# Expert weights loaded in four large ring parts with 32 KB and 16 KB runs, in place of twelve slots with 8 KB runs

## The reference, cut to what matters

```python
D_MODEL, N_EXPERTS, TOP_K, D_EXPERT = 1024, 32, 4, 1024

def encoder_layer(x, ...):
    h = rms_norm(x, norm_mix_g)
    mix, ... = token_mixers(h, ...)          # gated delta rule || conformer convolution, then w_out
    x = x + mix
    h = rms_norm(x, norm_ffn_g)
    return x + moe_ffn(h, ...)

def moe_ffn(h, w_router, b_router, w_gate_up, b_gate_up, w_down, b_down):
    logits = h @ w_router + b_router
    top_val, top_idx = lax.top_k(logits, TOP_K)
    gates = softmax(top_val)
    ...                                      # for each expert e, on its rows xblk of h:
        gu = xblk @ w_gate_up[e] + b_gate_up[e]      # w_gate_up[e]: 1024 x 2048 f32, 8 MB
        x_glu, x_lin = split(gu, 2)
        x_glu, x_lin = minimum(x_glu, 7.0), clip(x_lin, -7.0, 7.0)
        act = x_glu * sigmoid(1.702 * x_glu) * (x_lin + 1.0)
        y = act @ w_down[e] + b_down[e]              # w_down[e]: 1024 x 1024 f32, 4 MB
    ...                                      # y, times the gate, is added to the rows it belongs to
```

## Time and profile before

| | |
|---|---|
| median of 3 runs | 1297.71 us (1296.84 to 1298.78) |
| profiled execution | 1296.87 us, its span 1295.1 us |
| PE busy in the span | 1197.0 us (92%) |
| HBM read | 428.50 MB, 402.65 MB of it weights of experts |
| weight loads | 256 of w_gate_up and 128 of w_down, 1024 KB each |
| mean granted TensorE clock | 0.977 of 2.4 GHz |

### The profile page before, as it was taken

The page is one execution under the profiler, slowest core; times in us unless marked ns, Lnnn a source line. Parts: engine busy times, 40 slices in busy tenths (PEclk is TensorE's granted clock), DMA queues, the critical chain, the costliest instruction groups (busy, mean ns, idle before and its releaser), DMA issues. The chain is left out here.

```text
span 1295.1 us, 17190 instructions
## 1 busy us (share of the span) xinstructions
PE 1197.0 (92%) x6556; PEld 560.7 (43%) x6556; DVE 451.3 (35%) x887; ACT 241.8 (19%) x426; POOL 78.7 (6%) x81
## 2 busy tenths in 40 slices
PE   6999979998999999999999899899999999998986
PEld 3666669855543433323232324434343332323332
DVE  2989633224553223231312222321323322131224
ACT  2134425323201101010111101011110101111012
POOL 1100144154000000000000000000000000000000
PEclk9989989798899999999999999999999999999999
DMA  9321210016999999999999999999999999999994
GB/s 377 152 86 72 87 25 2 9 58 256 395 380 420 421 422 422 421 422 423 422 422 422 421 422 421 393 363 421 422 422 422 422 422 422 423 422 421 420 422 202
DMA packets 62153, 433.76 MB, mean 335 GB/s; under 512 B 7744, under 2 KB 8128, under 8 KB 11968
## 3 DMA queue, kind: packets, MB, share of 16 engines
q1 hardware_dynamic: 59696, 428.65, 80.4%
q0 software_dynamic: 800, 3.08, 0.6%
q10 hardware_dynamic: 1616, 1.45, 0.4%
HBM read 428.50 MB, written 4.65 MB: 334 GB/s over the span
## 5 line engine op out<-in xcount | busy, mean ns | idle before, releaser
L1835 PE MATMUL bank<-ring,win 128*64 128x512 f32 x1984 | 451.6, 599 | 44.9 <-DMA ring<-in_w_gate_up 44.9
L1835 PEld LDWEIGHTS bank<-ring,win 128*64 128x64 f32 x1984 | 135.0, 137 | 343.9 <-issue 206.6
L1855 PE MATMUL bank<-ring,win 128*64 128x512 f32 x992 | 222.6, 602 | 0.3 <-issue 0.3
L1303 DVE TENSOR_SCALAR win<-bank 128x512 f32<-128x512 f32 x33 | 22.8, 691 | 408.6 <-PE bank L1835 386.7
L1855 PEld LDWEIGHTS bank<-ring,win 128*64 128x64 f32 x992 | 70.3, 138 | 134.3 <-issue 131.1
L802 ACT ACTIVATE win<-win 128x512 f32<-128x512 f32 x33 | 20.8, 630 | 453.9 <-DVE win L1303 453.9
L810 ACT ACTIVATE win<-bank 64x512 f32<-64x512 f32 x64 | 37.8, 591 | 280.7 <-PE bank L1855 266.5
L1816 PE MATMUL bank<-qkvc,win 128*128 128x512 bf16 x288 | 67.7, 380 | 1.9 <-DVE xt L1297 1.9
L1237 DVE TENSOR_TENSOR win<-win,qkvc 128x1024 f32<-128x1024 f32 x16 | 19.6, 1226 | 143.0 <-ACT qkvc L828 143.0
L1297 DVE TENSOR_TENSOR xt<-xt,bank 128x512 f32<-128x512 f32 x108 | 68.0, 681 | 2.7 <-PE bank L1810 2.1
L937 DVE SCALAR_TENSOR_TENSOR cb<-ring,par,cb 128x384 f32<-128x384 f32 x120 | 66.7, 611 | 0.8
(11 more groups left out here) (305 smaller groups left out, 1083.0 us busy)
## 6 DMA issues: line engine op xcount, KB each, us to landing
ring<-in_w_gate_up SPq DMA_DIRECT2D x256, 1024.0 KB, 25.9
ring<-in_w_down SPq DMA_DIRECT2D x128, 1024.0 KB, 23.5
win<-in_w_in SPq DMA_DIRECT2D x3, 2048.0 KB, 7.3
ring<-in_w_in SPq DMA_DIRECT2D x2, 2048.0 KB, 13.5
win<-in_w_out SPq DMA_DIRECT2D x2, 2048.0 KB, 8.6
win<-in_w_in SPq DMA_DIRECT2D x4, 512.0 KB, 10.5
out_ss<-ring POOLq DMA_DIRECT2D x1, 2048.0 KB, 9.4
hT<-in_xT SPq DMA_DIRECT2D x2, 768.0 KB, 6.8
```

The lines of the kernel that those rows point to most:

```text
L1303: dve.tensor_scalar(g_s, bank[low], LIMIT, None, ALU.min).then_inc(g, 1)
L1835: mm = pe.matmul(bank[half][a * BLK:(a + 1) * BLK], xs[:, k], ring[:, c:c + 512], start=False, stop=(k == KD - 1), skip_group_check=True)
L1855: mm = pe.matmul(bank[7][a * BLK:(a + 1) * BLK], actT[:, (k % 4) * P + (k // 4) * BLK:][:, 0:BLK], ring[:, c:c + 512], start=(k == 0), sto ...
```

## The change

The ring is cut into four parts in place of twelve slots: two gate-up parts of 4 MB (4 slots each) and two down parts of 2 MB (2 slots each). A partition's rows in a part are neighbours in HBM: part r of gate-up holds rows r x 512 to r x 512 + 511, and partition p has rows 4p to 4p + 3 of them, a run of 32 KB. A down part has 4 rows of 4 KB in each partition, a run of 16 KB. There is one load for each part, one landing semaphore and one release. Expert 0 is loaded in six pieces (`FIRST_PIECES`), in the places of the ring and in the order of before; `EXTRA` counts them in the waits. The last part of the last expert is loaded in two halves, the second with a semaphore of its own.

Since row group k is now every fourth row of 512, the other operand must be picked in the same way. `h_parts` are written in the new order by ACT and DVE, which read h with a step of 16 bytes (`h2q`); `first_rows` reads h itself in this way; `a_rows` steps by 16 bytes, where it stepped by 8.

```diff
-SLOT_OF = (6, 7, 5, 0, 1, 2, 3, 4, 8, 9, 10, 11)
-FIRST_ORDER = (0, 1, 2, 8, 9, 3, 4, 5, 6, 7, 10, 11)
+GU, DN = 2, 2
+GQ, DQ = KD // GU, KD // DN
+NPART = GU + DN
+PART_AT = tuple(x * SLOT for x in (4, 0, 8, 10))
+FIRST_PIECES = ((0, 1, 4), (2, 0, 4), (1, 0, 2), (1, 2, 4), (0, 0, 1), (3, 0, 4))
+EXTRA = [16 * (sum(x[0] == r for x in FIRST_PIECES) - 1) for r in range(NPART)]
...
+        h2q = h2.rearrange("p (n r x q) -> p n r q x", n=NT, r=GU, q=GQ)
-        a_rows = a_s.rearrange("p (b r two) -> p b r two", b=2, two=2)
+        a_rows = a_s.rearrange("p (r q) -> p q r", q=DQ)
...
-        USED = (1, 2, 3, 4, 5, 6, 7, 11, 12, 13, 14, 16)
-        USES, GATE_UP_DONE, DOWN_DONE = 16, 11, 16
+        USED = [r + 1 for r in range(GU - 1)] + [GU + 3, GU + 4, GU + 6]
+        USES, GATE_UP_DONE, DOWN_DONE = GU + 6, GU + 3, GU + 6
...
+            def load_piece(ld, e, r, q0, q1, done=None):
+                if r < GU:
+                    rows_of, width, src = GQ, 2 * F, w_gate_up[bass.ds(e, 1), r * GQ * P:(r + 1) * GQ * P, :]
+                else:
+                    rows_of, width = DQ, D
+                    src = w_down[bass.ds(e, 1), (r - GU) * DQ * P:(r - GU + 1) * DQ * P, :]
+                src = src.rearrange("a (p q) n -> (a p) (q n)", q=rows_of)
+                ld.dma_start(ring[:, PART_AT[r] + q0 * width:PART_AT[r] + q1 * width], src[:, q0 * width:q1 * width])\
+                  .then_inc(done or s_w[r], 16)
+            def load_expert(ld, e, value):
+                for r in range(NPART):
+                    ld.wait_ge(s_wu, value(r))
+                    load_piece(ld, e, r, 0, GQ if r < GU else DQ)
...
-                            mm = pe.matmul(out, h_parts[j][:, n, k * P:(k + 1) * P], hits[:, n, 0:width],
+                            mm = pe.matmul(out, h_parts[j][:, n, k // GQ, k % GQ], hits[:, n, 0:width],
...
-                                       h23[:, n, k * P:(k + 1) * P], hp0[:, n], start=(n == 0), stop=(n == NT - 1))
+                                       h2q[:, n, k // GQ, k % GQ], hp0[:, n], start=(n == 0), stop=(n == NT - 1))
...
                 for k in range(KD):
-                    pe.wait_ge(s_w[SLOT_OF[k]], turn * 16 + 16)
+                    r, q = divmod(k, GQ)
+                    if q == 0:
+                        pe.wait_ge(s_w[r], turn * 16 + (16 + EXTRA[r]))
...
-                    if k < KD - 1:
+                    if q == GQ - 1 and k < KD - 1:
                         mm.then_inc(s_wu, 1)
```

More of the change, by code:

```diff
@@ L311, in stream_step @@
         s_tabs = sem("tables_ready")
-        s_w = [sem(f"w_landed{i}") for i in range(NSLOT)]
-        s_wu = sem("w_used")
+        s_w = [sem(f"w_landed{i}") for i in range(NPART)]
+        s_wu, s_whalf = sem("w_used"), sem("w_landed_last_half")
         s_xg4, s_xg5, s_xt4, s_xt5 = (sem(x) for x in ("rows_gathered_low", "rows_gathered_high", "rowsT_low", "rowsT_high"))
@@ L467, in _ @@
                             load_expert(sp, ei, lambda s: i * USES + ((NE - 4) * USES + USED[s]))
-            for e in (NE - 3, NE - 2, NE - 1):
+            for e in (NE - 3, NE - 2):
                 number = sp.value_load(expert_no[0:1, e:e + 1], min_val=0, max_val=NE - 1)
                 load_expert(sp, number, lambda s: n_extra * USES + ((e - 1) * USES + USED[s]))
+            number = sp.value_load(expert_no[0:1, NE - 1:NE], min_val=0, max_val=NE - 1)
+            for r in range(NPART):
+                sp.wait_ge(s_wu, n_extra * USES + ((NE - 2) * USES + USED[r]))
+                load_piece(sp, number, r, 0, GQ if r < GU else DQ // 2 if r == NPART - 1 else DQ)
+            load_piece(sp, number, NPART - 1, DQ // 2, DQ, s_whalf)
             for n in TILES:
@@ L817, in h_split @@
                 for n in TILES:
-                    act.activation(h_parts[0][:, n], h23[:, n], ACT.Copy).then_inc(s_up, 1)
+                    act.activation(h_parts[0][:, n], h2q[:, n], ACT.Copy).then_inc(s_up, 1)
                 act.wait_ge(s_lg, NT)
@@ L821, in h_split @@
                     act.wait_ge(s_lo, n + 1)
-                    act.activation(h_parts[1][:, n], h23[:, n], ACT.Copy).then_inc(s_up, 1)
+                    act.activation(h_parts[1][:, n], h2q[:, n], ACT.Copy).then_inc(s_up, 1)
             def y_split(u):
@@ L1844, in turn_act, with down @@
                 for j in range(4):
-                    mm = pe.transpose(bank[6][:, j * P:(j + 1) * P], a_rows[:, j // 2, :, j % 2], mat("ident"))
+                    mm = pe.transpose(bank[6][:, j * P:(j + 1) * P], a_rows[:, j], mat("ident"))
                 mm.then_inc(done, 1)
-            def down(turn, atr, n_atr):
+            def down(turn, atr, n_atr, last=False):
                 pe.wait_ge(atr, n_atr)
                 for k in range(KD):
-                    if k % 2 == 0:
-                        pe.wait_ge(s_w[KD + k // 2], turn * 16 + 16)
+                    j, q = divmod(k, DQ)
+                    if q == 0:
+                        pe.wait_ge(s_w[GU + j], turn * 16 + (16 + EXTRA[GU + j]))
+                    if last and k == KD - DQ // 2:
+                        pe.wait_ge(s_whalf, 16)
                     for a in range(2):
-                        c = (KD + k // 2) * SLOT + (k % 2) * D + a * 512
-                        mm = pe.matmul(bank[7][a * BLK:(a + 1) * BLK], actT[:, (k % 4) * P + (k // 4) * BLK:][:, 0:BLK],
+                        c = PART_AT[GU + j] + q * D + a * 512
+                        mm = pe.matmul(bank[7][a * BLK:(a + 1) * BLK], actT[:, q * P + j * BLK:][:, 0:BLK],
                                        ring[:, c:c + 512], start=(k == 0), stop=(k == KD - 1), skip_group_check=True)
@@ L1858, in down @@
                             mm.then_inc(s_wu, 1)
-                    if k % 2 == 1 and k < KD - 1:
+                    if q == DQ - 1 and k < KD - 1:
                         mm.then_inc(s_wu, 1)
@@ L1927, in wide_unit @@
                 for k in range(KD):
-                    pe.wait_ge(s_w[SLOT_OF[k]], WIDE * 16 + 16)
+                    r, q = divmod(k, GQ)
+                    if q == 0:
+                        pe.wait_ge(s_w[r], WIDE * 16 + 16 + EXTRA[r])
                     for x in range(2):
@@ L1931, in wide_unit @@
                             for a in range(2):
-                                c = SLOT_OF[k] * SLOT + half * F + a * 512
+                                c = PART_AT[r] + q * SLOT + half * F + a * 512
                                 mm = pe.matmul(bank[4 * x + half][a * BLK:(a + 1) * BLK], xTe[:, k, x * BLK:(x + 1) * BLK],
@@ L2019, in _ @@
             turn_hits(hp, BLK)
-            down(turn, s_atr, item + 1)
+            down(turn, s_atr, item + 1, last=True)
             pe.wait_ge(s_gtc, NU)
```

45 lines of the change are left out of this document (18 added, 27 removed).

## The result

The changed kernel takes 1304.18 us (median of 13 runs, 1300.06 to 1307.23) against 1297.71 (13 runs, 1294.72 to 1298.95): **a ratio of 1.0055, 95% interval 1.0044 to 1.0066**, 6.5 to 7.1 us slower. Its profiled execution took 1301.27 us with a span of 1299.5 (before 1296.87 and 1295.1). That one lies in the lower part of its runs, so the two traces show 4.4 us of the difference, and what the other runs had more is in no trace.

What follows compares the result with a forecast made beforehand. The stream of weights was taken as the bound, in a chain with PE through expert 16 and PE's tail. The end 6.2 us late plus 0.9 for the clock, 7.1 us on the median 1297.71, gave 1304.8 us; range 1297 to 1312.

Steps and rivals of the forecast that it cites:

- Long runs: Weight streams: 32 KB runs at 431.5 GB/s, 0.6 us saved per expert, 16.2 us over 27 experts.
- (a) Expert 0's start: First gate-up: stepped reads in first_rows cost 4.3 us (0 to 6.8), covering a 0.8 us late landing; start at 337.5.
- (b) Expert 1: Experts 1 and 2: parts freed and landed later, all of expert 2 at 409.4 against 403.5; start phase loses 5.9 us.
- (c), (d) The wide expert: Expert 16 starts 4.5 us later, at 801.1; the stream stands about 17 us against 8, losing its 2.5 us lead.
- The stop that was to be seen about 840: Sign to look for at the wide expert: a stop of 10 us in the GB/s line.
- (e) The end: Last weights land at 1267.7, four rows remain for PE, gate-up ends at 1274.6: 6.2 us late, same tail behind.
- (f) The clock: After long waits PE's clock may halve; counted only at experts 15 and 31, 0.9 us, range 0 to 3.6.
- Some 28 waits of 2 to 3 us, more in total than 44.9: Sign to look for: PE's waits at gate-up's second part, in place of 83 short waits totalling 44.9 us.
- stepped reads are not free: Denies the rival that stepped reads of h cost nothing, which gave 1300.3 us; chance 0.23.
- a rate of 435: Rival in the streams: long runs cost nothing of their own, 434.9 GB/s, 8.4 us less, 1296.4 us; chance 0.12.
- 32 KB runs are single packets: Denies a case of the does-less rival: runs cut into 16 KB packets, +4 us; that rival's chance 0.14.
- the distance in HBM: Rival in gate-up loads: partitions reading 32 KB apart cost 3.6 us an expert, about 1400 us; chance 0.03.

Runs made afterwards that it cites:

- short_coarse: Changed kernel with its parts, waits and releases, but each transfer cut by rows into 8 KB runs; 1319.19 us, 1.0180 of the kernel before.
- contig: Changed kernel with first_rows reading h without the 16-byte step (some values then wrong); 1300.64 us, 1.0030 of the kernel before.
- short_fine: Changed kernel's row order and stepped reads, but twelve 1 MB pieces per expert with 8 KB runs, waited for and released singly; 1301.46 us, 1.0042 of the kernel before.
- start: Changed kernel with 1 MB pieces in experts 0 and 1, no step in first_rows, release by 1 MB; 1300.13 us, 1.0032 of the kernel before.
- wide: Changed kernel with 1 MB pieces in experts 0 and 15 to 18, their pair 17/18 written out, release by 1 MB; 1299.34 us, 1.0027 of before.
- mix: Changed kernel with 1 MB pieces in experts 0, 1, 15 to 18, 31, no step in first_rows, 17/18 written out; 1294.50 us, 0.9982 of before.
- mix3: mix with expert 30 also in 1 MB pieces and a second pair of experts written out ahead of the loop; 1289.51 us, 0.9951 of the kernel before.

## Why the prediction was right

The forecast was 1304.8 us, the median 1304.18. The chain of costs and its places are borne out by the experiments. That the number is met to within 1 us is luck in part: for the two traces that the working is about it was 2.7 us too high (7.1 against 4.4), and within it several errors cancel. Step by step:

- **Long runs.** 431.5 GB/s was extrapolated for 32 KB; the changed kernel's windows show 431 and 430. The gain of 16.2 us was measured as 16.2 between short_coarse and the changed kernel. The intervals of the two ratios (1.0164 to 1.0196 and 1.0044 to 1.0066) leave some 2.5 us to either side of that.
- **(a) Expert 0's start.** first_rows took 11.47 us in place of 7.17, the 4.3 that was chosen between 0 and 6.8. It started 1.4 us earlier than in the trace of before, so gate-up began at 336.50 instead of 337.5. The two ways to measure the step's price at the end give 3.2 (contig) and 5.4 us (short_fine), each with an uncertainty of some 2. The size was met by luck, for the reading behind it does not hold. The 0.157 us between the starts of the transposes is raised by the first of each four, whose matmul takes 385 ns where the others take 284; the others start 0.121 apart, against 0.110 for the plain rows, so 0.011 and not 0.047 was there to be doubled. And the doubling does not come: the four transposes of 16-byte rows (L1861) still take 0.75 us, so 0.2 us for each group should have been 0. What first_rows pays is 0.12 us a pass at full clock, and it comes to 4.3 only because a third of the passes ran at half clock in the kernel before, where the step adds 0.02. The passage of the Trainium skill that the prediction names ("SBUF — State Buffer", section "Door 1: The DMA port swizzle") has lines of 16 bytes and two reads of a line for full rate, and goes on to call a stride of 4 fp32 free, which is 16 bytes. By the first part 8 bytes are free and 16 pay, by the second 16 are free: at full clock first_rows agrees with the first (329 ns against 192) and contradicts the second. The transposes, 0.121 at both steps, show no further cost from 8 to 16 bytes; whether it is the step at all that sets them apart from the plain rows, no run isolates.
- **(b) Expert 1.** Landings at 356.8 (forecast 356.6) and, for expert 2's part 0, 390.4 (389.9). Both hide two errors each. Expert 0's gate-up began 1.0 us early, but TensorE was at half clock again at its start (0.50 in 336.5:338; 15.13 us in place of 13.90), so its first part was freed at 344.6, not 344.4. Expert 1's gate-up began at 369.12, 1.6 us before the 370.7 forecast, but the load behind it took 14.0 us from issue to landing where 12.2 were worked out. 4.7 us of stream were missing by 460 where 5.9 less the first gain, about 5, were forecast. Without the step the coarse parts alone cost little here, 1.7 us by short_coarse against short_fine and nothing measurable by start against contig.
- **(c), (d) The wide expert.** It started at 800.05 (forecast 801.1) and expert 17 at 855.14 (856.8). By the bytes moved in 780:900 (404 and 332 GB/s, two windows of 60 us) the stream stood 120 - 44.2 MB / 431 = 17.5 us, as forecast, against 7 us before (417 and 379; the forecast had 8). The stop that was to be seen about 840, 10 us long, is there: from 839 to 849 next to nothing moves. The two windows of the changed kernel:

```profile
780.00:840.00 60.00, 56.01 (x374) 25.14 (x376) 17.71 (x31) 5.78 (x8) 0.00 (x0) 1.00 0.96 404
840.00:900.00 60.00, 59.42 (x356) 23.70 (x354) 15.26 (x29) 8.39 (x13) 0.00 (x0) 1.00 0.81 332
```

- **(e) The end.** Expert 31's part 1 landed at 1265.7, 2.0 us earlier than forecast, and gate-up ended at 1273.0 instead of 1274.6; 4.4 late, not 6.2. Of the 2.0, 1.5 is that expert 17 freed its part earlier. The tail behind it is the same, as forecast: the last down ends at 1285.2 us, 12.2 behind the end of gate-up, and in the kernel before at 1280.8, also 12.2; from the landing of the last weights it is 9.7 us (forecast 11) and was 4.3 (the forecast had 6). The whole forecast of the trace (7.1) was thus 2.7 too high, 1.8 of it here and 0.9 in the clock, and the runs' medians lie closer to it than the trace does.
- **(f) The clock.** 0.9 us were put in for a chance of a fall at experts 15 and 31. Neither had one (expert 15's second half took 7.09 us). Falls are there in the streams: of 13 waits of 2.0 to 2.65 us ten were followed by a half gate-up of 8.5 to 8.8 us instead of 7.09, and none of the ten waits of 1.31 us or less was. One of them, behind a wait of 2.56 us, came at expert 30, and its down was slow too (8.79), which the prediction did not think of. The 3.4 us then cost only the 0.5 by which PE was later than the landing. One window:

```profile
1236.50:1240.00 3.50, 3.49 (x10) 1.06 (x12) 0.00 (x0) 0.00 (x0) 0.00 (x0) 0.52 0.97 412
```

- **What was wrong without harm.** "Some 28 waits of 2 to 3 us, more in total than 44.9": it was 23, of which 13 were of 2.0 to 2.65 us, 40.8 us in all. The two experts of a pair are not alike for PE, so long and short waits mostly go in turn, and where the clock falls behind a long one, 1.7 us of the next wait are used up. The period of two experts is 1031.56 - 973.11 = 58.45 us, forecast 58.5:

```profile
973.11 8.78 PE L1851 MATMUL bank<-ring,win 128*64 128x512 f32 x32 [2.63 <-DMA ring<-in_w_gate_up]
...
1002.33 7.09 PE L1851 MATMUL bank<-ring,win 128*64 128x512 f32 x32 [0.57 <-DMA ring<-in_w_gate_up]
...
1031.56 8.79 PE L1851 MATMUL bank<-ring,win 128*64 128x512 f32 x32 [2.64 <-DMA ring<-in_w_gate_up]
```

The rivals: stepped reads are not free; the length of a run does matter, so a rate of 435 did not come; 32 KB runs are single packets; and the distance in HBM costs nothing that short_fine could show. On the last, with partitions 32 KB apart and 8 KB runs the rate is 422 GB/s, as before. The figures behind the rule that the prediction cites (the Trainium skill, "DMA: Bandwidth & Descriptors", "Latency and other measured facts") are for row pitches from 512 KiB up, so these runs, at 32 KB, neither bear it out nor contradict it.

## What to carry to other kernels

A stream of weights gains from long runs only while it is the bound; the places where it stands still and where it ends pay for the size of its parts. Size the parts by place: long runs in the steady stretch, small pieces for the loads behind which compute ends and for those around a stop. And a layout that makes runs long changes who reads with a step: look for the reader on the path.

## What the runs showed of the hardware

- A 32 KB run goes as one packet. Rates of three lengths: 422 GB/s at 8 KB, 428 at 16 KB, 431 at 32 KB: each doubling gives about half of the one before, as a fixed cost of some 9 ns a run would have it. The packets' own times are 314, 615 and 1217 ns.
- The fp32 weight loads of first_rows with elements 16 bytes apart take 329 ns at both clock levels; with adjacent elements they take 333 at half clock and 192 at full clock. The transposes' loads did not change between 8 and 16 bytes (210 ns).
- The same loop exit cost PE 1.6 to 2.2 us in ten kernels and 7.8 and 8.0 us in two. Two loads of instructions stand there in all twelve; PE goes on with the first in the ten and with the second in the two. The long wait cost 3 to 4 us by the spans (wide against the changed kernel 3.4; mix against mix3 3.9, with expert 30's pieces in it), as much as small pieces at one place give.
